# Order and queues of the first input transfers in a two-block transformer kernel on one core

## The reference, cut to what matters

```
c_act = silu(c)
mod   = c_act @ w_ada[0] + b_ada[0]          # shift, scale, ...
h     = rms_norm(x, norm1[0]) * (1 + sc1) + sh1
proj  = h @ w_in[0]                          # the first weight tiles
# rotary: ang = positions * inv_freq; cos(ang), sin(ang)
```

## Time and profile before

| what | value |
|---|---|
| median of 3 runs | 3226.9 us (3226.77 to 3227.86) |
| profiled execution, span from first to last instruction | 3225.6 us |
| PE busy in that span | 3207.7 us (99%) |
| DVE, ACT, POOL busy | 59%, 36%, 7% |
| granted clock of TensorE, mean | 0.999 |
| read from memory | 354 MB, 110 GB/s over the span |

### The profile page before, as it was taken

The page is one execution under the profiler, slowest core; times in us unless marked ns, Lnnn a source line. Parts: engine busy times, 40 slices in busy tenths (PEclk is TensorE's granted clock), DMA queues, the critical chain, the costliest instruction groups (busy, mean ns, idle before and its releaser), DMA issues.

```text
span 3225.6 us, 43771 instructions
## 1 busy us (share of the span) xinstructions
PE 3207.7 (99%) x15424; PEld 2655.3 (82%) x15424; DVE 1898.1 (59%) x2745; ACT 1158.9 (36%) x1533; POOL 239.3 (7%) x249
## 2 busy tenths in 40 slices
PE   8999999999999999999999999999999999999998
PEld 7788888888888788888888888768888888878887
DVE  8455567564447455667564445666665744586656
ACT  4433333332223433243332223354333523553423
POOL 2100000100001100000100002051000101320001
PEclk9999999999999999999999999999999999999999
DMA  7146325422222156424422222203322322122222
GB/s 259 66 159 207 129 93 168 142 95 96 98 98 92 60 162 201 139 87 164 146 98 98 97 93 94 79 27 98 104 96 94 109 95 94 49 79 98 98 98 78
DMA packets 100059, 357.84 MB, mean 111 GB/s; under 512 B 11328, under 2 KB 13648, under 8 KB 99808
## 3 DMA queue, kind: packets, MB, share of 16 engines
q1 hardware_dynamic: 99248, 353.99, 32.9%
q0 software_dynamic: 688, 2.21, 0.2%
HBM read 354.06 MB, written 2.10 MB: 110 GB/s over the span
## 4 chain that ended last, share of the span: by engine, by line
PE 98%; DVE 1%; ACT 0%; DMA 0%; DVEq 0%; issue 0%; ACTq 0%; POOL 0%; POOLq 0%; SPq 0%
PE pb L622 25%; PE pb L623 25%; PE pb L624 25%; PE pb L654 2%; PE pb L655 2%; PE pb L658 2%; PE pb L702 2%; PE pb L701 2%; PE pb L700 2%; PE pb L1024 1%; PE pb L1400 1%; PE pb L1401 1%; PE pb L1402 1%; PE pb L931 1%; PE pb L1014 1%; PE pb L932 1%
## 5 line engine op out<-in xcount | busy, mean ns | idle before, releaser
L1472 ACT ACTIVATE hi<-raw 128x1024 fp32r<-128x1024 f32 x548 | 575.8, 1056 | 979.2 <-PE pb L624 678.0
L2013 DVE TENSOR_TENSOR lo<-raw,hi 128x1024 fp32r<-128x1024 f32 x548 | 667.7, 1223 | 356.1 <-ACT hi L1472 310.8
L622 PE MATMUL pb<-yH,hi 128*128 128x512 f32 (+1 forms) x1664 | 644.8, 388 | 0.0
L624 PE MATMUL pb<-yH,lo 128*128 128x512 f32 (+1 forms) x1664 | 644.6, 387 | 0.0
L623 PE MATMUL pb<-yL,hi 128*128 128x512 f32 (+1 forms) x1664 | 644.6, 387 | 0.0
L622 PE MATMUL pb<-hH,hi 128*128 128x512 f32 x1512 | 590.6, 391 | 0.0
L623 PE MATMUL pb<-hL,hi 128*128 128x512 f32 x1512 | 589.0, 390 | 0.0
L624 PE MATMUL pb<-hH,lo 128*128 128x512 f32 x1512 | 588.9, 389 | 0.0
L622 PEld LDWEIGHTS pb<-yH,hi 128*128 128x128 f32 x1664 | 312.7, 188 | 63.6
L623 PEld LDWEIGHTS pb<-yL,hi 128*128 128x128 f32 x1664 | 312.7, 188 | 63.5
L624 PEld LDWEIGHTS pb<-yH,lo 128*128 128x128 f32 x1664 | 312.7, 188 | 63.1
(11 more groups left out here) (433 smaller groups left out, 4041.2 us busy)
## 6 DMA issues: line engine op xcount, KB each, us to landing
raw<-stream SPq DMA_DIRECT2D x648, 512.0 KB, 3.3
yF<-first SPq DMA_DIRECT2D x8, 512.0 KB, 13.0
act<-first SPq DMA_DIRECT2D x8, 512.0 KB, 15.9
x<-xT SPq DMA_DIRECT2D x4, 512.0 KB, 7.8
outT<-act SPq DMA_DIRECT2D x7, 256.0 KB, 2.2
tab<-decay SPq DMA_DIRECT2D x1, 1024.0 KB, 6.4
scr<-ws POOLq DMA_DIRECT2D x2, 256.0 KB, 3.0
scr<-bs POOLq DMA_DIRECT2D x2, 256.0 KB, 3.4
```

What stands on the lines that cost most here:

```text
L622: pe.matmul(out, whi, ahi, start=first, stop=False)
L624: return pe.matmul(out, wlo, ahi, start=False, stop=last)
L1472: act.activation(hi[:, s], raw[:, s], ACT.Copy).then_inc(hi_ready, 1)
L2013: dve.tensor_tensor(lo[:, s, 0:width], raw[:, s, 0:width], hi[:, s, 0:width].bitcast(F32), ALU.subtract).then_inc(lo_ready, 1)
```

## The change

`x`'s four transfers become the first that SP issues. The four small ones (`c`, positions, small columns, identity and ones) are issued by ACT, ahead of everything else in its list. POOL issues `v2` only after its seven remainders, just before the tables of the spatial gating. DVE's wait for `v2` moves to where the table is first read. Nothing is computed otherwise than before.

```
@@ SP
-            sp.dma_start(cs[:, 0], cvec).then_inc(c_in, 16)
-            sp.dma_start(scr[:, 0:S].bitcast(I32), pos).then_inc(pos_in, 16)
-            sp.dma_start(cst[:, C_EDGE:C_ALL], consts[:, C_EDGE:C_ALL]).then_inc(freq_in, 16)
-            sp.dma_start(cst[:, 0:C_FOLD], consts[:, 0:C_FOLD]).then_inc(setup_in, 16)
             for n in range(4):
                 sp.dma_start(x[:, 2 * n:2 * n + 2], xT[:, 2 * n:2 * n + 2]).then_inc(x_in[n], 16)
@@ POOL
             pool.dma_start(v1[:], vec1).then_inc(vec1_in, 16)
-            pool.dma_start(v2[:], vec2).then_inc(vec_in, 16)
...
                 pool.drain().then_inc(h_pool, 1)
+            pool.dma_start(v2[:], vec2).then_inc(vec_in, 16)
@@ ACT
+            act.dma_start(cs[:, 0], cvec).then_inc(c_in, 16)
+            act.dma_start(scr[:, 0:S].bitcast(I32), pos).then_inc(pos_in, 16)
+            act.dma_start(cst[:, C_EDGE:C_ALL], consts[:, C_EDGE:C_ALL]).then_inc(freq_in, 16)
+            act.dma_start(cst[:, 0:C_FOLD], consts[:, 0:C_FOLD]).then_inc(setup_in, 16)
             act.wait_ge(c_in, 16)
@@ DVE
-            dve.wait_ge(vec_in, 16)
             hr.next(KT)
...
                 else:
+                    dve.wait_ge(vec_in, 16)
                     dve.tensor_tensor(gain2[:], v2[:, W_FIN1:W_FIN1 + 8], v2[:, W_MIX:W_MIX + 8], ALU.mult)
```

More of the change, by code:

```diff
@@ L421, in into_place @@
                     sp.dma_start(first_at(m), first[m]).then_inc(first_in[m], 16)
[L423 to L426, removed]
             for n in range(4):
```

## The result

The changed kernel takes 3231.9 us (median of 21 runs, 3231.1 to 3233.1). The kernel before, run beside it, takes 3227.75 us (21 runs, 3226.8 to 3229.1). The ratio is 1.0013, with a 95% interval of 1.0008 to 1.0019: 4.1 us slower, by less than 0.2% but clear of the scatter. The forecast was 3227.8 with a range up to 3229.6, so the time is above the range. Within 0.2%, and slower rather than faster, held; the size did not.

The account below looks back on a forecast made before the run. PE bounds the kernel, with the head set by the later of PE's and DVE's chains to the root. PE's +0.9 us outweighed DVE's +0.2, giving a span of 3226.5 and a median of 3227.8 us, range 3225.0 to 3229.6.

Parts of the forecast that it names:

- What bounds the head: Before the root: PE's and DVE's chains end within 0.2 us of each other; the later decides and passes to the end.
- always 10.34: PE's list from its first product to ACT's root: claimed always 10.34 us if DVE's sums are in time.
- x's squares and the additions without idle: Head: squares end about 9.9, 4.4 us earlier, worth nothing alone; six additions without waits take 4.54 us.
- v2 away from the beginning: Start of the head: without v2, identity and ones would land about 5.1, a gain of 2.0 us on PE's chain.
- The positions then land at 1.27 + 2.8 + about 1.0 = 5.0: ACT's queue, taking turns with x: positions land at 5.0, small columns at 6.4, identity and ones at 8.0.
- the forecast's full turn: Both queues at the start: 128 rows of a small transfer let 128 rows of x pass, 1.29 us.
- near 4.2: SP's queue: x's first transfer, issued at 0.8, lands like a ring tile alone, 3.3 us after issue.
- The bounds: Landings of positions, small columns, identity: 4.0, 4.4, 5.1 without x in the way; 8.6, 8.8, 9.1 behind all of x.
- Rival C: Head: x's full queue served first, DVE's chain +2.6 us, 3229.5 us; chance 0.17.
- A: Head: queues take turns, +0.9 us, between 0 and +1.8, 3226.9 to 3228.7 us; the forecast, chance 0.50.
- v2 and DVE's wait at their new places: POOL after its remainders: later tables issued 0.54 us later, hidden by 73.8 us of idling; DVE's wait costs zero.

Follow-up runs that it names:

- v2_late: Kernel before with only v2's issue moved behind POOL's remainders and DVE's wait for it moved; 3227.1 us, ratio 0.9997.
- c_twice: Changed kernel with c sent a second time on ACT's queue, into an unused column, ahead of the positions; 3232.9 us.
- c_on_sp: Changed kernel with c (4 KB, 128 rows) moved from ACT's queue to the front of SP's; 3229.1 us.
- x_half_rows: Changed kernel with x in eight transfers of 256 KB, rows of 2 KB instead of 4 KB; 3229.2 us, ratio to before 1.0004.
- one_queue: Changed kernel with all on SP's queue: x's four, then c, positions, small columns, identity and ones; ACT issues nothing; 3232.9 us.
- split_small: v2_late with c and positions on ACT's queue, small columns and identity and ones on SP's ahead of x; 3225.6 us, ratio to before 0.9993.
- tile_first: split_small with one w_ada tile (512 KB) put ahead of x on SP's queue; 3230.9 us in a single execution.

## Why the prediction was wrong, by its own steps

- *What bounds the head.* Right. Two chains, PE from identity and ones (10.34 us to the root, now 21.14 - 11.34 = 9.80) and DVE from the small columns (9.55 us forecast to the last addition, measured 19.35 - 9.65 = 9.70). Both moved, and the end moved with the root, +3.7, without loss or gain on the way. The 0.5 us by which PE's chain was shorter are its first products: 16 in 3.39 us for 3.78, and the first fillers, 3.35 for 3.50. The forecast's "always 10.34" does not hold: 9.80 to 11.31 in the kernels of the table.
- *x's squares and the additions without idle.* Right in what they are worth: the additions run without idle time, and nothing else was gained. The squares end at 11.9 (10.72 + 1.15), not at the forecast 9.9, since x's last landed at 10.7 and not at 8.7. ACT's last two squares in the changed kernel:

```profile
10.72 1.15 ACT L1522 ACTIVATE act<-x 128x512 f32<-128x512 f32 x2 [0.45 <-DMA x<-xT]
```

- *v2 away from the beginning.* Over-priced: 2.0 us forecast for identity and ones, 0.9 measured alone (v2_late). The 51 GB/s between 4.5 and 5.0 were read as v2's doing; the stretch is as slow without it.
- *The step that failed:* "The positions then land at 1.27 + 2.8 + about 1.0 = 5.0". They landed at 8.2. The forecast counted turns for the positions, the small columns and identity, and none for `c`, because it has 4 KB; I costed silu at 4.3 from ACT's issue times alone (its fourth issue took 1.10 us and not 0.42, but that was hidden: ACT then waited another 1.05 for `c`). `c` has 128 rows and landed at 5.7, and the positions stood behind it. Of the 3.2 us, c's turn is an estimated 1.0 to 1.3 (what another `c` cost in c_twice, and the forecast's full turn), the late first transfer of x 1.4 (next point), and some 0.6 to 0.8 are not told apart. The other two terms of the same sum were well sized: small columns 9.65 - 8.21 = 1.4 behind the positions (forecast 1.4), identity 11.29 - 9.65 = 1.6 (forecast 1.6). c_on_sp, c_twice and x_half_rows show the mechanism: it was forecast, and one row of its sum was left out.
- *A second term, mis-sized:* x's first at "near 4.2", from the 3.3 us of a tile in the steady stream. It landed at 5.6, and at 5.0 with no company (one_queue). With rows passing at 201 GB/s instead of 407, each early turn costs twice as much. The stretches of the changed kernel, last three columns clock, DMA share, GB/s:

```profile
3.00:5.00 2.00, 0.00 (x0) 0.00 (x0) 0.00 (x0) 1.28 (x1) 0.00 (x0) 1.00 0.64 201
5.00:7.00 2.00, 0.00 (x0) 0.00 (x0) 0.00 (x0) 1.24 (x3) 0.00 (x0) 1.00 1.00 403
```

- *The bounds.* Rival C, all of x ahead, was meant as the worst case: x done at 8.0, small columns at 8.8, identity at 9.1. It has no turn of `c` in it; it fell by x's slow start, since one_queue, which does put all of x ahead, had them at 9.2, 10.2 and 10.5. And it was no bound: with turns, identity landed later still, at 11.3. The range fell with it. The 4.1 us are also less than the 6.5 that the forecast took as the least one can tell from no change, and they stand clear of the scatter. The sign and the class came out as forecast; C's mechanism (x goes wholly ahead) is not what happened, A's is, with four turns instead of three and a slow start.
- *v2 and DVE's wait at their new places.* Right, zero: POOL's select moved from 49.15 to 53.81, and POOL still idled 73.4 us behind it (73.8 before).

The page "DMA: Bandwidth & Descriptors" of the Trainium skill (section "Queues, rings and completion order") has the DMA engines go round between the queue rows packet by packet, and gives a packet as typically about 9 to 17 descriptors. The runs agree with turns, but not with that size: here a turn was one row of each queue, as the hand-overs show (131 against 15), and the measurement decides.

## What to carry to other kernels

A small transfer on a second queue does not run beside a large one that has rows waiting: it takes turns with it row by row, so price it by its rows times the other queue's row, not by its bytes, and count every transfer ahead of it in its own queue, the 4 KB ones too. What the first instructions wait for belongs ahead of the bulk; in split_small two queues helped by 1.4 us (medians), with small rows on both and the bulk behind them. And the steady-state time of a transfer is too low a price for the first one of a program (3.3 us against 4.2 to 4.7).

## What the runs showed of the hardware that was not expected

- x's first rows are slow at the start of the program, in one queue or two: 215 GB/s from 2 to 4 us in one_queue and 201 from 3 to 5 in the changed kernel, against 403 to 410 right after. The cause is open.
- PE's first 16 products took 3.78 us in the kernel before and 3.39 in the changed one; the filler products of the same width behind them take 0.11 us each (30 in 3.35). Before the 0.11 they take 0.2 us and more each, for 3.4 us in the changed kernel and longer in others (the 30 fillers took 3.51 us there and 4.68 in split_small, by PE's timeline). The granted clock in the rows is 1.00 all through. PE had been idle until then in every profile.
- The last operation of the inverse root (128x4) took 2.28 us in one_queue and 2.27 in tile_first, 0.16 in the other twelve profiles. Not explained.
